# Odd layer of a two-block model: values and gates in one 512-column product, and the queries of the next pair moved

## The chip, the cores and the metric

The kernel runs on one core of one Trainium2 chip. The metric is the device time of one execution in microseconds (us); less is better. A core has TensorE (PE) for matrix products, VectorE (DVE) and ScalarE (ACT) for elementwise work, GpSimd (POOL), and SyncE (SP), which here only issues the loads of weights. PE has two rows in a trace, PE for the products and PEld for the loading of their stationary operands.

## The reference, cut to what matters

A first block (attention, feed-forward, gated embedding) is followed by two layers on 256 tokens of `x` and 256 tokens of a context. The change is in the second of these, the odd layer:

```python
zf_l, zb_l, i_l, q_l, g_l = jnp.split(h_lat @ w_in, idx, axis=-1)      # x's tokens: 5 x 2048 columns
zf_c, zb_c, i_c = jnp.split(h_ctx @ w_in[:, :idx[2]], idx[:2], axis=-1)  # context: 3 x 2048
for lb, z_l, z_c, reverse in ((lb_fwd, zf_l, zf_c, False), (lb_bwd, zb_l, zb_c, True)):
    k, logf = hgrn2_gates(z, lb)              # both token sets
    s_ctx = hgrn2_final_state(k_c, v_c, lf_c, s0)
    o_l, _ = hgrn2_chunk_scan(q_l, k_l, v_l, lf_l, s_ctx)
o = o * lax.rsqrt(jnp.mean(o * o, axis=-1, keepdims=True) + EPS)
return (o.reshape(b, n, HG_V) * onorm_g * jax.nn.silu(g)) @ w_out
```

There are 16 heads of 128 columns. Queries `q` and gates `g` are needed for the tokens of `x` alone, values `v` and the two forget projections `zf` and `zb` for both sets.

## The kernel before, in words

Everything is float32. A weight is split into a rounded part `whi` and a rest `wlo`, an activation into `h` and `l`, and a product is the sum of three (high by high, low by high, high by low), each a PE instruction with a 128x128 stationary operand.

**Chunks.** `Plan` lays the whole program out as a list of chunks of 1024 weight columns per partition (512 KB). SyncE loads a chunk into one of 5 `raw` buffers. ACT makes `whi` from it (L1152), DVE makes `wlo` (L1746), PE multiplies. There are 4 buffers of each, and the loops of ACT and DVE run with PE's: in their iteration for chunk c (`Engine.chunks`) they first split chunk c+3, and ACT's part of that waits until PE has finished chunk c-1. Then they call `pump()`.

**Pumps.** Small work that lies beside the products is written as generators that advance by one step at each `pump()`. PE calls `pump()` before each chunk, and in groups whose products cover 512 tokens also before each further 128 rows of the weight (L706 ff.). ACT and DVE call it once for each chunk, and a second time in such groups. In the odd layer `serial` is set, so that only the first generator of the list advances. A generator's waits on semaphores stand in the engine's own queue: what is behind them waits too.

**The odd layer** goes through 8 pairs of heads, j = 0 to 7. A group is one projection of a pair:

- `q` and `g`: 256 weight columns, x's 256 tokens moving: 96 products of 256 columns, 4 chunks
- `v` (token-major, activations stationary, weights moving): 4 blocks of 128 tokens, 192 products of 256 columns, 4 chunks
- `zf`, `zb`: 512 tokens moving, 96 products of 512 columns each, 4 chunks

The order is q0 g0 v0 zf0 zb0, then q, v, zf, g, zb for j = 1 to 7, then `w_out` in groups o0 to o3. Sums stand in PSUM banks 0 to 3, in two alternating sets. Bank 4 takes transposes and scores, 5 and 6 the states of the two heads (`ds`), 7 the outputs.

**Beside the products** runs `direction(j, d)`. It starts when `zf` (d = 0) or `zb` (d = 1) of the pair is complete. ACT takes sigmoids (L1688, L1689), then in its pumps logarithms (pump 1, L1321), exponentials (pump 3, L1329 to L1332), copies of the transposes (pumps 7 and 9, L1342). DVE scans in pump 2 (L2058 to L2071), makes the decayed keys in pump 4 (L2076, L2078, semaphore `kd`), and masks scores and combines states in pumps 8 and 10 (L2096 to L2104, semaphores `scm`, `ss`). PE's part has the steps `(9 if n else 10, 2 if d else 3, 2, 2, 3)` with n = 2j + d:

```python
        def turn(h):
            e.wait_ge(S("kd"), n + 1)
            if h:
                e.wait_ge(S("scm"), 2 * n + 1)
```

so for d = 1 `turn(0)` (L918) comes in PE's pump 10, `states(0)` (L933) in 12, `turn(1)` in 14, `outputs(0)` (L948) with `states(1)` in 16, `outputs(1)` in 19. For d = 0 they come in 10, 13, 15, 17, 20. Direction (7, 1) has steps of its own and runs in o0 and o1.

`readout(j)` follows in the next pair's `zf`: ACT squares (L1359) and takes a root (L1363), DVE a reciprocal (L2119), ACT scales the outputs into `OT` (L1368, its pump 3), PE transposes them (L977, seventh pump), DVE multiplies by norm and gate (L2127), ACT and DVE make the high and low part (L1372, L2131).

Of the kernel before, what the change touches and what calls it, by code (L numbers as in the profile page):

```python
# [13 lines left out]
D = 2048  # L14
T = 256
# [43 lines left out]


class Group:
    pass


class Plan:
# [55 lines left out]
    def modulate(self, W):

# [43 lines left out]
def schedule(A):  # L166
# [54 lines left out]
    p.rate = 0.0  # L221
    W = A["od_w_in"]
    for j in range(8):
        p.group(f"q{j}", W, 6144 + 256 * j, 256, NT, T)
        if j == 0:
            p.group(f"g{j}", W, 8192 + 256 * j, 256, NT, T)
        p.group(f"v{j}", W, 4096 + 256 * j, 256, NT, 2 * T, tm=True)
        p.group(f"zf{j}", W, 256 * j, 256, NT, 2 * T)
        if j > 0:
            p.group(f"g{j}", W, 8192 + 256 * j, 256, NT, T)  # L230
        p.group(f"zb{j}", W, 2048 + 256 * j, 256, NT, 2 * T)
    W = A["od_w_out"]
    for g in range(2):
# [71 lines left out]
class Memory:  # L305


    def __init__(self, nc, A):
# [132 lines left out]
        self.X1 = Turned(self, "half", cut(self.HCh, 0, T), cut(self.HCl, 0, T), True, hn, t)  # L441
        self.X1c = Turned(self, "half", cut(self.HCh, T, N), cut(self.HCl, T, N), True, hn, t)
        self.hV = self.sb("hV", [128, 4, 256], F32, F)
        self.hQ = self.sb("hQ", [128, 2, T], F32, F + 28)
        self.hG = self.sb("hG", [128, 2, T], F32, F + 30)
        self.hA = self.sb("hA", [128, 2, N], F32, F + 4)
        self.hB = self.sb("hB", [128, 2, N], F32, F + 8)
        self.hC = self.sb("hC", [128, 2, N], F32, F + 12)
# [50 lines left out]
        return self.LB[:, 32 + 16 * d + k:33 + 16 * d + k]  # L499

    def ds(self, h, n):
        return self.PS[5 + h][:, 128 * n:128 * n + 128]


class Engine:
# [18 lines left out]
    def chunks(self, name, prep=None, ahead=0, upto=None):  # L524

        G = self.plan.by[name]
        for j, ch in enumerate(G.chunks[:upto]):
            if prep is not None:
                prep.upto(min((G.j0 + j + 1) * G.kt - 1 + ahead, G.K - 1))
            self.upto(ch.c)  # L530
            self.pump()
            if self.serial and G.N == 512:
                self.pump()
            self.modulate(ch)
        return G
# [144 lines left out]
class Tensor(Engine):  # L680
# [80 lines left out]
    def modulate(self, ch):  # L761
# [12 lines left out]
        for l in ch.turns:  # L774
            self.ada_turn(l)

    def ada_turn(self, b):
        m, S, e = self.m, self.S, self.e
        e.wait_ge(S("ada_R"), b + 1)
        for i in range(4):  # L780
            t = e.transpose(m.PS[6 + b][:, 128 * i:128 * i + 128], m.R[b][:, 128 * i:128 * i + 128], m.ident)
        t.then_inc(S("ada_tr"), 1)
# [115 lines left out]
    def direction(self, j, d):  # L898
# [14 lines left out]
            elif d:  # L913
                e.wait_ge(S("scm"), 2 * n)
            elif j:
                e.wait_ge(S("og"), j)
# [65 lines left out]
def tensor(m, e):  # L982
# [93 lines left out]
    XQ = P.turned(m.X1)  # L1076
    works, reads = [], []
    for j in range(8):
        P.group(f"q{j}", XQ)
        if j == 0:  # L1080
            first = []
# [19 lines left out]
        P.group(f"v{j}", X)  # L1101
# [6 lines left out]
        if j:  # L1108
            P.group(f"g{j}", XQ)
# [29 lines left out]
class Scalar(Engine):  # L1139
# [211 lines left out]
    def readout(self, j):  # L1351
# [11 lines left out]
        e.activation(m.SM[:, 4:8], m.SM[:, 4:8], ACT.Sqrt).then_inc(S("rr"), 1)  # L1363
        yield
        yield
        e.wait_ge(S("ri"), j + 1)
        for i in range(4):
            a = e.activation(m.OT[:, i, :], m.PS[7][:, 128 * i:128 * i + 128], ACT.Copy, scale=m.SM[:, 4 + i:5 + i])  # L1368
        a.then_inc(S("ot"), 1)
        yield  # L1370
        e.wait_ge(S("og"), j + 1)
        e.activation(m.OH[:, 2 * j:2 * j + 2, :], m.hG[:, :, :], ACT.Copy).then_inc(S("oh"), 1)  # L1372
        yield


def scalar(m, e):
# [285 lines left out]
    def queries(j):  # L1662
        G = P.chunks(f"q{j}", X1, 2)
        e.wait_ge(S("mm"), G.done)
        if j:
            e.wait_ge(S("qd"), 2 * j)
        e.activation(m.hQ[:, :, :], PS[G.base][:, :], ACT.Copy).then_inc(S(f"set{G.s}"), 1)

    def gates(j):
        G = P.chunks(f"g{j}", X1, 2)  # L1670
        if j == 0:
            P.finish()
            X1c.upto(2)
        e.wait_ge(S("mm"), G.done)
        if j:
            e.wait_ge(S("ol"), j)
        e.activation(m.hG[:, :, :], PS[G.base][:, :], ACT.Sigmoid).then_inc(S("gs"), 1)

    def forget(j, d):
        n = 2 * j + d  # L1680
# [10 lines left out]

    works, reads = [], []
    for j in range(8):
        queries(j)
        if j == 0:
            P.beside = [rest()]
            gates(0)
# [39 lines left out]
class Vector(Engine):  # L1737
# [307 lines left out]
    def direction(self, j, d):  # L2045
# [68 lines left out]
    def readout(self, j):  # L2114
# [2 lines left out]
        e.tensor_scalar(m.SM[:, 4:8], m.SM[:, 0:4], 1.0 / 128, EPS, ALU.mult, ALU.add).then_inc(S("rm"), 1)  # L2117
        e.wait_ge(S("rr"), j + 1)
        e.reciprocal(m.SM[:, 4:8], m.SM[:, 4:8]).then_inc(S("ri"), 1)  # L2119
        yield  # L2120
        yield
        yield
        e.wait_ge(S("otr"), j + 1)
        G = self.plan.by[f"g{j}"]
        e.wait_ge(S(f"set{G.s}"), G.freed)
        for h in range(2):
            t = e.scalar_tensor_tensor(m.hG[:, h, :], m.PS[4][:, 256 * h:256 * h + 256], m.v("onorm", 2 * j + h),  # L2127
                                       m.hG[:, h, :], ALU.mult, ALU.mult)
        t.then_inc(S("og"), 1)
        e.wait_ge(S("oh"), j + 1)  # L2130
        e.tensor_tensor(m.OL[:, 2 * j:2 * j + 2, :], m.hG[:, :, :], m.OH[:, 2 * j:2 * j + 2, :].bitcast(F32),  # L2131
                        ALU.subtract).then_inc(S("ol"), 1)
        yield


def vector(m, e):
# [366 lines left out]
    def gates(j):
        G = P.chunks(f"g{j}")
        if j == 0:
            P.finish()
            X1c.upto(2)
        e.wait_ge(S("gs"), j + 1)
        e.tensor_tensor(m.hG[:, :, :], PS[G.base][:, :], m.hG[:, :, :], ALU.mult).then_inc(S(f"set{G.s}"), 1)

    works, reads = [], []
    for j in range(8):
        P.chunks(f"q{j}", X1, 2)
        if j == 0:
            e.wait_ge(S("ld_cx"), 32)
# [17 lines left out]
        works, reads = [P.direction(j, 1)], [P.readout(j)]
# [110 lines left out]
```

## Time and profile before

| | |
|---|---|
| median of 3 runs | 3124.61 us (3124.38 to 3124.99) |
| the profiled execution | 3124.67 us, its span 3122.9 us |
| PE busy | 3083.2 us, 99% of the span, 16978 products |
| DVE, ACT busy | 64%, 46% |
| mean share of the DMA engines, last third | 0.3 to 0.4 |
| odd layer, pair j = 3 (q3's start at 2521.57 to zb3's end) | 99.6 us |

The span is the stretch between the first and last record. PE's busy time includes modelled ends of products, so PE's pace is read from distances between starts. A row on a stretch has its bounds and length in us, the busy time and number of instructions of PE, PEld, DVE, ACT and POOL, TensorE's granted clock as a share of full speed, the DMA share and GB/s. A timeline row has start (us), duration (us), engine, line, operation, output<-inputs, shapes, and in brackets the engine's idle time before it and what ended that. An "xN" at the end of a timeline row stands for N instructions merged into it, each of which starts before the next row does. Weights of the odd layer arrive in 3.5 us a chunk.

### The profile page before, as it was taken

The numbers are of one execution on the slowest core, as the hardware profiler recorded it, in microseconds if no ns is written. First come the engines' busy times: TensorE is split into PE (matmuls) and PEld (weight loads), VectorE is DVE, ScalarE is ACT, GpSimd is POOL, SyncE is SP. The second block draws the span as 40 slices with busy tenths as digits, with TensorE's granted clock in tenths as the row PEclk, the third lists the DMA queues.
The fourth block names the chain that finished last, engine by engine and source line by source line (L and its number), as shares of the span: only waits on it lengthen the run. The fifth ranks groups of instructions, "written<-read, shape, count | busy, mean of one in ns | idle before, by whom it ended". The sixth has DMA issues, their size and how long they took to land.

```text
span 3122.9 us, 41500 instructions
## 1 busy us (share of the span) xinstructions
PE 3083.2 (99%) x16978; PEld 2666.3 (85%) x16978; DVE 1998.3 (64%) x2502; ACT 1422.3 (46%) x2029; POOL 97.3 (3%) x74
## 2 busy tenths in 40 slices
PE   8999999999999999999999999999999999999998
PEld 8989888888888888878888888888889999899987
DVE  6767777789888887857877755442743444443455
ACT  5344555465555554436422222232644544444454
POOL 0000003001111100000000000000000000000000
PEclk9999999999999999999999999999999999999999
DMA  8776666757667677775556555342333333333334
GB/s 302 231 248 216 208 212 216 250 179 230 213 221 225 216 251 266 254 240 197 161 170 191 178 193 179 127 150 95 103 96 104 100 108 114 102 110 97 112 131 146
DMA packets 369982, 557.59 MB, mean 179 GB/s; under 512 B 17088, under 2 KB 239296, under 8 KB 368512
## 3 DMA queue, kind: packets, MB, share of 16 engines
q1 hardware_dynamic: 366784, 540.08, 53.6%
q0 software_dynamic: 2000, 12.06, 1.0%
q8 instruction: 134, 2.20, 0.3%
q10 hardware_dynamic: 1008, 2.80, 0.2%
q14 instruction: 56, 0.46, 0.0%
HBM read 552.64 MB, written 2.23 MB: 178 GB/s over the span
## 4 chain that ended last, share of the span: by engine, by line
PE 95%; DVE 2%; ACT 1%; issue 1%; DMA 1%; ACTq 0%; DVEq 0%
PE ps L736 91%; DVE wlo L1746 1%; PE ps L933 0%; PE ps L948 0%; PE ps L938 0%; PE ps L950 0%; ACT whi L1152 0%; PE ps L807 0%; DMA CX<-in_ctx 0%; PE ps L771 0%; DVE HCl L1900 0%; PE ps L861 0%; PE ps L845 0%; PE ps L918 0%; PE ps L935 0%
## 5 line engine op out<-in xcount | busy, mean ns | idle before, releaser
L1746 DVE TENSOR_TENSOR wlo<-raw,whi 128x1024 fp32r<-128x1024 f32 (+1 forms) x823 | 1013.4, 1235 | 822.5 <-ACT whi L1152 820.6
L1152 ACT ACTIVATE whi<-raw 128x1024 fp32r<-128x1024 f32 x828 | 869.9, 1057 | 1166.5 <-PE ps L736 1150.3
L736 PE MATMUL ps<-HCh,whi 128*128 128x512 f32 (+1 forms) x1816 | 508.2, 361 | 0.0
L736 PE MATMUL ps<-HCh,wlo 128*128 128x512 f32 (+1 forms) x1816 | 500.8, 357 | 0.0
L736 PE MATMUL ps<-HCl,whi 128*128 128x512 f32 (+1 forms) x1816 | 500.3, 357 | 0.0
L736 PE MATMUL ps<-V,whi 128*128 128x512 f32 x1408 | 445.2, 398 | 0.8 <-DVE V L1902 0.8
L1763 DVE SCALAR_TENSOR_TENSOR acc<-raw_ada,S,acc 128x1024 f32<-128x1024 f32 x330 | 436.4, 1334 | 5.0 <-DMA raw_ada<-in_ada_w 4.2
L736 PEld LDWEIGHTS ps<-HCh,wlo 128*128 128x128 f32 x1816 | 323.6, 189 | 49.8
L736 PEld LDWEIGHTS ps<-HCl,whi 128*128 128x128 f32 x1816 | 323.5, 189 | 49.8
L736 PEld LDWEIGHTS ps<-HCh,whi 128*128 128x128 f32 x1816 | 319.7, 190 | 49.7 <-issue 4.2
L736 PEld LDWEIGHTS ps<-V,wlo 128*128 128x128 f32 x1408 | 265.4, 188 | 62.8
L736 PE MATMUL ps<-V,wlo 128*128 128x256 f32 x1408 | 277.4, 278 | 0.0
L736 PEld LDWEIGHTS ps<-V,whi 128*128 128x128 f32 x1408 | 215.2, 189 | 2.7 <-issue 1.7
L736 PE MATMUL ps<-whi,HCh 128*128 128x256 f32 (+1 forms) x896 | 197.7, 336 | 1.5 <-DVE HCl L1939 1.5
L736 PE MATMUL ps<-wlo,HCh 128*128 128x256 f32 (+1 forms) x896 | 191.5, 329 | 0.0
L736 PE MATMUL ps<-whi,HCl 128*128 128x256 f32 (+1 forms) x896 | 191.3, 329 | 0.0
L736 PEld LDWEIGHTS ps<-wlo,HCh 128*128 128x128 f32 x896 | 142.7, 190 | 15.3
L736 PEld LDWEIGHTS ps<-whi,HCl 128*128 128x128 f32 x896 | 142.4, 190 | 15.2
L736 PEld LDWEIGHTS ps<-whi,HCh 128*128 128x128 f32 x896 | 139.9, 190 | 14.7 <-issue 1.9
L736 PE MATMUL ps<-whi,Uh 128*128 128x512 f32 x384 | 121.3, 397 | 0.0
L736 PE MATMUL ps<-whi,Ul 128*128 128x512 f32 x384 | 118.6, 390 | 0.0
L736 PE MATMUL ps<-wlo,Uh 128*128 128x512 f32 x384 | 118.4, 390 | 0.0
(345 smaller groups left out, 3484.5 us busy)
## 6 DMA issues: line engine op xcount, KB each, us to landing
raw_ada<-in_ada_w SPq DMA_DIRECT2D x192, 512.0 KB, 4.8
raw<-in_w_up SPq DMA_DIRECT2D x176, 512.0 KB, 4.3
raw<-in_w_in SPq DMA_DIRECT2D x160, 512.0 KB, 4.0
raw<-in_od_w_in SPq DMA_DIRECT2D x160, 512.0 KB, 3.5
raw<-in_ev_w_in SPq DMA_DIRECT2D x96, 512.0 KB, 3.8
raw<-in_w_down SPq DMA_DIRECT2D x88, 512.0 KB, 5.1
raw<-in_w_out SPq DMA_DIRECT2D x32, 512.0 KB, 4.8
raw<-in_w_ple_gate SPq DMA_DIRECT2D x32, 512.0 KB, 4.6
```

What stands on the lines that cost most here:

```text
L736: mm = e.matmul(o, a, b, start=first and t == 0, stop=last, skip_group_check=True)
L1152: e.activation(m.whi[ch.i % SPLIT][:, 0:n], m.raw[ch.slot][:, 0:n], ACT.Copy).then_inc(S("hi"), 1)
L1746: e.tensor_tensor(m.wlo[ch.i % SPLIT][:, 0:n], m.raw[ch.slot][:, 0:n], m.whi[ch.i % SPLIT][:, 0:n].bitcast(F32), ALU.subtract).then_inc(S( ...
L1763: t = e.scalar_tensor_tensor(m.acc[v][:, :], w, c, m.acc[v][:, :], ALU.mult, ALU.add)
```

## The change

- For j = 1 to 7 `g` and `v` become one group (`Plan.pair`, PE's `values`) of 8 chunks of 256 weight rows by 512 columns, from an input `od_w_vg` in which the host has put the values' and the gates' columns of a pair side by side. For each 128 rows PE makes 6 products of 512 columns for x's tokens (values and gates) and 6 of 256 for the context's (values). The context's sums stand in bank 6, and both heads' states in bank 5.
- The gates are now token-major, so DVE multiplies the outputs by reciprocal and gate as it fills `OT`, before the transposes. ACT and DVE then apply the norm as they read the transposes.
- Group `q` of pair j + 1 stands where `g` of pair j stood; the order is q0 g0 v0 zf0 q1 zb0, then v, zf, q of the next pair, zb. After zf7 there is no such group.
- `hQ` and `hG` have two buffers each.
- `direction`'s steps are as before.

```diff
+            p.pair(f"v{j}", A["od_w_vg"], j)
         p.group(f"zf{j}", W, 256 * j, 256, NT, 2 * T)
-        if j > 0:
-            p.group(f"g{j}", W, 8192 + 256 * j, 256, NT, T)
+        if j < 7:
+            p.group(f"q{j + 1}", W, 4096 + 256 * (j + 1), 256, NT, T)
         p.group(f"zb{j}", W, 2048 + 256 * j, 256, NT, 2 * T)
...
-            if self.serial and G.N == 512:
+            if self.serial and G.N == 512 and (j % 2 or not G.pair):
                 self.pump()
...
+    def values(self, j, X):
...
+        for i, ch in enumerate(G.chunks):
+            self.pump()
+            e.wait_ge(S("lo_dve"), ch.n_lo)
...
+            for k in range(2):
+                kk = 2 * i + k
+                if k:
+                    self.pump()
+                for t in range(3):
+                    for b in range(2):
+                        e.matmul(m.PS[G.base + b][:, :], (X.lo if t == 1 else X.hi)(kk)[:, 128 * b:128 * b + 128],
+                                 ws[t == 2][:, k, :], start=kk == t == 0, stop=kk == NT - 1 and t == 2,
+                                 skip_group_check=True)
+                if i % 2 and not k:
+                    self.pump()
+                for t in range(3):
+                    for b in range(2):
+                        mm = e.matmul(m.PS[6][:, 256 * b:256 * b + 256],
```

ACT behind group `v`, and DVE's part that waits for it:

```diff
+            for b in range(2):
+                e.activation(m.hV[:, b, :], PS[G.base + b][:, 0:256], ACT.Copy)
+            e.activation(m.hV[:, 2:4, :], PS[6][:, :], ACT.Copy)
+            if j > 1:
+                e.wait_ge(S("ol"), j - 1)
+            for b in range(2):
+                a = e.activation(m.hG[j % 2][:, b, :], PS[G.base + b][:, 256:512], ACT.Sigmoid)
+            a.then_inc(S("gs"), 1)
...
+            e.wait_ge(S("gs"), j + 1)
+            for b in range(2):
+                t = e.tensor_tensor(m.hG[j % 2][:, b, :], PS[G.base + b][:, 256:512], m.hG[j % 2][:, b, :], ALU.mult)
+            t.then_inc(S(f"set{G.s}"), 1)
```

The readout, ACT's part and then DVE's:

```diff
-        e.wait_ge(S("ri"), j + 1)
-        for i in range(4):
-            a = e.activation(m.OT[:, i, :], m.PS[7][:, 128 * i:128 * i + 128], ACT.Copy, scale=m.SM[:, 4 + i:5 + i])
-        a.then_inc(S("ot"), 1)
...
+        e.wait_ge(S("otr"), j + 1)
+        for h in range(2):
+            a = e.activation(m.OH[:, 2 * j + h, :], m.PS[4][:, 256 * h:256 * h + 256], ACT.Copy,
+                             scale=m.v("onorm", 2 * j + h))
...
+        for i in range(4):
+            h, p = divmod(i, 2)
+            t = e.scalar_tensor_tensor(m.OT[:, i, :], m.PS[7][:, 128 * i:128 * i + 128], m.SM[:, 4 + i:5 + i],
+                                       m.hG[j % 2][:, p, 128 * h:128 * h + 128], ALU.mult, ALU.mult)
+        t.then_inc(S("ot"), 1)
...
+        e.wait_ge(S("oh"), j + 1)
         for h in range(2):
+            t = e.scalar_tensor_tensor(m.OL[:, 2 * j + h, :], m.PS[4][:, 256 * h:256 * h + 256],
+                                       m.v("onorm", 2 * j + h), m.OH[:, 2 * j + h, :].bitcast(F32), ALU.mult,
+                                       ALU.subtract)
```

## Rows read from the trace of the kernel before

**Rows 1.** Stretches, busy time by engine: one pair, then two behind or around waits.

```profile
2521.57:2621.20 99.63, 99.63 (x665) 91.75 (x664) 42.66 (x72) 46.46 (x69) 0.00 (x0) 1.00 0.34 106
...
632.10:638.70 6.60, 5.87 (x23) 5.05 (x22) 6.22 (x10) 4.17 (x8) 0.00 (x0) 0.50 0.24 69
...
3061.40:3068.20 6.80, 5.27 (x25) 4.11 (x24) 3.93 (x5) 2.63 (x3) 0.00 (x0) 1.00 0.49 164
```

**Rows 2.** Timeline of PE, end of g2 and first half of zb2.

```profile
2487.73 0.40 PE L736 MATMUL ps<-HCh,whi 128*128 128x256 f32 x2
...
2494.69 0.40 PE L736 MATMUL ps<-HCl,whi 128*128 128x256 f32 x2
2494.93 0.63 PE L736 MATMUL ps<-HCh,whi 128*128 128x512 f32 x2
...
2501.30 0.62 PE L736 MATMUL ps<-HCl,whi 128*128 128x512 f32 x2
```

**Rows 3.** Timeline of ACT from the end of zb2.

```profile
2521.77 0.60 ACT L1688 ACTIVATE hC<-ps 128x512 f32<-128x512 f32 x1 [7.29 <-PE ps L736]
...
2533.55 0.63 ACT L1329 ACTIVATE hKI<-hB 128x512 f32<-128x512 f32 x1 [2.73 <-DVE TS L2071]
...
2535.22 1.04 ACT L1152 ACTIVATE whi<-raw 128x1024 fp32r<-128x1024 f32 x1
```

**Rows 4.** Timeline of DVE in the same stretch.

```profile
2536.30 1.23 DVE L1746 TENSOR_TENSOR wlo<-raw,whi 128x1024 fp32r<-128x1024 f32 x1 [1.65 <-ACT whi L1152]
...
2538.63 0.48 DVE L2078 SCALAR_TENSOR_TENSOR hA<-hC,LB,hA 128x256 f32<-128x256 f32 x1
...
2544.81 0.35 DVE L2096 TENSOR_SCALAR hST<-ps,DEC 128x128 f32<-128x128 f32 x1 [1.07 <-PE ps L938]
2545.08 0.41 DVE L2097 TENSOR_TENSOR hSC<-ps,hgm 128x256 int32<-128x256 int32 x1
```

**Rows 5.** Timeline of PE: turn(0) of direction (2, 1), and states(0).

```profile
2540.29 0.38 PE L918 MATMUL ps<-cst,hA 128*128 128x128 f32 x2
...
2543.49 0.61 PE L933 MATMUL ps<-hV,hB 128*128 128x128 f32 x4
```

**Rows 6.** Timelines, direction (0, 0) inside zb0 (ACT, DVE, PE).

```profile
2293.86 0.60 ACT L1688 ACTIVATE hC<-ps 128x512 f32<-128x512 f32 x1 [4.32 <-PE ps L736]
...
2305.92 0.48 DVE L2078 SCALAR_TENSOR_TENSOR hA<-hC,LB,hA 128x256 f32<-128x256 f32 x1
...
2312.09 0.71 PE L933 MATMUL ps<-hV,hB 128*128 128x128 f32 x4 [0.23 <-ACT hB L1342]
...
2321.27 0.49 PE L948 MATMUL ps<-hST,hQD 128*128 128x128 f32 x2 [1.30 <-DVE hST L2104]
```

**Rows 7.** Timelines of ACT, DVE, PE, readout in zf3 (zf3's first product at 2560.78).

```profile
2560.98 1.09 ACT L1704 ACTIVATE hV<-ps 128x512 f32<-128x512 f32 x2 [5.53 <-PE ps L736]
...
2564.06 1.28 ACT L1363 ACT_TABLE_LOAD   x1
2565.36 0.21 ACT L1363 ACTIVATE SM<-SM 128x4 f32<-128x4 f32 x1
...
2565.60 0.18 DVE L2119 RECIPROCAL SM<-SM 128x4 f32<-128x4 f32 x1 [1.24 <-ACT SM L1363]
...
2568.97 0.60 PE L977 MATMUL ps<-cst,hOT 128*128 128x128 f32 x4
```

**Rows 8.** Timeline of PE, its waits in o0 to o1b.

```profile
3037.42 0.44 PE L918 MATMUL ps<-cst,hA 128*128 128x128 f32 x2 [1.11 <-DVE hA L2078]
...
3066.30 0.70 PE L736 MATMUL ps<-whi,Oh 128*128 128x512 f32 x2 [1.53 <-DVE Ol L2131]
```

**Rows 9.** Timeline of PE, waits before clock drops.

```profile
631.38 0.99 PE L807 MATMUL ps<-cst,H 128*128 128x128 f32 x6 [2.85 <-DVE H L2259]
...
2212.08 1.30 PE L807 MATMUL ps<-cst,hnf 128*128 128x128 f32 x6 [1.94 <-DVE hnf L1888]
2214.67 0.66 PE L807 MATMUL ps<-cst,hnf 128*128 128x128 f32 x2 [1.29 <-DVE HCl L1900]
```

More of the change, by code:

```diff
@@ L61 @@
 class Group:
-    pass
+    pair = False
 class Plan:
@@ L119, in group, with pair @@
         return G
+    def pair(self, name, W, j):
+        G = Group()
+        G.cols, G.K, G.kt, G.N, G.tm, G.raw, G.wide, G.first = 512, NT, 2, 2 * T, True, False, False, True
+        G.j0, G.j1, G.pair = 0, 8, True
+        G.s = self.sets % 2
+        self.sets += 1
+        G.use = self.uses[G.s]
+        self.uses[G.s] += 1
+        G.freed, G.base = G.use + 1, 2 * G.s
+        G.chunks = []
+        for i in range(8):
+            rows = W[i * 256:(i + 1) * 256, 512 * j:512 * j + 512]
+            G.chunks.append(self.stream(rows.rearrange("(k p) c -> p k c", p=128), 2, 512, True, True))
+        G.done = G.chunks[-1].n
+        self.by[name] = G
     def modulate(self, W):
@@ L223, in schedule @@
     for j in range(8):
-        p.group(f"q{j}", W, 6144 + 256 * j, 256, NT, T)
         if j == 0:
-            p.group(f"g{j}", W, 8192 + 256 * j, 256, NT, T)
-        p.group(f"v{j}", W, 4096 + 256 * j, 256, NT, 2 * T, tm=True)
+            p.group("q0", W, 4096, 256, NT, T)
+            p.group("g0", A["od_w_vg"], 256, 256, NT, T, tm=True)
+            p.group("v0", A["od_w_vg"], 0, 256, NT, 2 * T, tm=True)
+        else:
+            p.pair(f"v{j}", A["od_w_vg"], j)
         p.group(f"zf{j}", W, 256 * j, 256, NT, 2 * T)
-        if j > 0:
-            p.group(f"g{j}", W, 8192 + 256 * j, 256, NT, T)
+        if j < 7:
+            p.group(f"q{j + 1}", W, 4096 + 256 * (j + 1), 256, NT, T)
         p.group(f"zb{j}", W, 2048 + 256 * j, 256, NT, 2 * T)
@@ L346, in __init__ @@
         at += 4 * ADA_SLOTS
+        self.acc_at = at
         self.acc = [self.sb(f"acc{v}", [128, 1024], F32, at + 4 * v) for v in range(2)]
@@ L443, in __init__ @@
         self.hV = self.sb("hV", [128, 4, 256], F32, F)
-        self.hQ = self.sb("hQ", [128, 2, T], F32, F + 28)
-        self.hG = self.sb("hG", [128, 2, T], F32, F + 30)
+        self.hQ = [self.sb(f"hQ{i}", [128, 2, T], F32, (F + 28, self.acc_at)[i]) for i in range(2)]
+        self.hG = [self.sb(f"hG{i}", [128, 2, T], F32, (F + 30, self.acc_at + 2)[i]) for i in range(2)]
         self.hA = self.sb("hA", [128, 2, N], F32, F + 4)
@@ L501, in ds @@
     def ds(self, h, n):
-        return self.PS[5 + h][:, 128 * n:128 * n + 128]
+        return self.PS[5][:, 256 * h + 128 * n:256 * h + 128 * n + 128]
 class Engine:
@@ L775, in modulate @@
             self.ada_turn(l)
+    def values(self, j, X):
+        m, S, e = self.m, self.S, self.e
+        G = self.plan.by[f"v{j}"]
+        e.wait_ge(S(f"set{G.s}"), G.use)
+        if j > 1:
+            old = self.plan.by[f"v{j - 1}"]
+            e.wait_ge(S(f"set{old.s}"), old.freed)
+        for i, ch in enumerate(G.chunks):
+            self.pump()
+            e.wait_ge(S("lo_dve"), ch.n_lo)
+            ws = [w[ch.i % SPLIT][:, :].rearrange("p (k c) -> p k c", k=2) for w in (m.whi, m.wlo)]
+            for k in range(2):
[12 more added lines that the diff above has]
+                        mm = e.matmul(m.PS[6][:, 256 * b:256 * b + 256],
+                                      (X.lo if t == 1 else X.hi)(kk)[:, T + 128 * b:T + 128 * b + 128],
+                                      ws[t == 2][:, k, 0:256], start=kk == t == b == 0,
+                                      stop=kk == NT - 1 and t == 2, skip_group_check=True)
+            mm.then_inc(S("mm"), 1)
     def ada_turn(self, b):
@@ L915, in turn @@
             elif j:
-                e.wait_ge(S("og"), j)
+                e.wait_ge(S("ol"), j)
             for i in range(2):
@@ L1078, in tensor @@
     for j in range(8):
-        P.group(f"q{j}", XQ)
         if j == 0:
+            P.group("q0", XQ)
             first = []
@@ L1100, in tensor @@
             X.turn = XC.turn
-        P.group(f"v{j}", X)
+            P.group("v0", X)
+        else:
+            P.values(j, X)
         P.finish(*works)
@@ L1107, in tensor @@
         P.beside += works
-        if j:
-            P.group(f"g{j}", XQ)
+        if j < 7:
+            P.group(f"q{j + 1}", XQ)
         P.group(f"zb{j}", X)
@@ L1365, in readout @@
         yield
-        e.wait_ge(S("ri"), j + 1)
-        for i in range(4):
-            a = e.activation(m.OT[:, i, :], m.PS[7][:, 128 * i:128 * i + 128], ACT.Copy, scale=m.SM[:, 4 + i:5 + i])
-        a.then_inc(S("ot"), 1)
         yield
-        e.wait_ge(S("og"), j + 1)
-        e.activation(m.OH[:, 2 * j:2 * j + 2, :], m.hG[:, :, :], ACT.Copy).then_inc(S("oh"), 1)
+        e.wait_ge(S("otr"), j + 1)
+        for h in range(2):
+            a = e.activation(m.OH[:, 2 * j + h, :], m.PS[4][:, 256 * h:256 * h + 256], ACT.Copy,
+                             scale=m.v("onorm", 2 * j + h))
+        a.then_inc(S("oh"), 1)
         yield
@@ L1664, in queries, with gates @@
         e.wait_ge(S("mm"), G.done)
[L1665 to L1673, printed above, removed]
+        if j > 1:
+            e.wait_ge(S("qd"), 2 * j - 2)
+        e.activation(m.hQ[j % 2][:, :, :], PS[G.base][:, :], ACT.Copy).then_inc(S(f"set{G.s}"), 1)
+    def gates():
+        G = P.chunks("g0", X1, 2)
+        P.finish()
+        X1c.upto(2)
         e.wait_ge(S("mm"), G.done)
-        if j:
-            e.wait_ge(S("ol"), j)
-        e.activation(m.hG[:, :, :], PS[G.base][:, :], ACT.Sigmoid).then_inc(S("gs"), 1)
+        e.activation(m.hG[0][:, :, :], PS[G.base][:, :], ACT.Sigmoid).then_inc(S("gs"), 1)
     def forget(j, d):
@@ L1693, in scalar @@
     for j in range(8):
-        queries(j)
         if j == 0:
+            queries(0)
             P.beside = [rest()]
-            gates(0)
+            gates()
         G = P.chunks(f"v{j}", X1c, 2)
@@ L1702, in scalar @@
             e.wait_ge(S("om"), 4 * j)
-        for i in range(2):
-            a = e.activation(m.hV[:, 2 * i:2 * i + 2, :], PS[G.base + i][:, :], ACT.Copy)
-        a.then_inc(S(f"set{G.s}"), 1)
+            for b in range(2):
+                e.activation(m.hV[:, b, :], PS[G.base + b][:, 0:256], ACT.Copy)
+            e.activation(m.hV[:, 2:4, :], PS[6][:, :], ACT.Copy)
+            if j > 1:
+                e.wait_ge(S("ol"), j - 1)
+            for b in range(2):
+                a = e.activation(m.hG[j % 2][:, b, :], PS[G.base + b][:, 256:512], ACT.Sigmoid)
+            a.then_inc(S("gs"), 1)
+        else:
+            for i in range(2):
+                a = e.activation(m.hV[:, 2 * i:2 * i + 2, :], PS[G.base + i][:, :], ACT.Copy)
+            a.then_inc(S(f"set{G.s}"), 1)
         forget(j, 0)
@@ L1709, in scalar @@
         P.beside += works
-        if j:
-            gates(j)
+        if j < 7:
+            queries(j + 1)
         forget(j, 1)
@@ L2082, in direction @@
         e.wait_ge(S(f"set{G.s}"), G.freed)
-        e.tensor_tensor(m.QD[:, :, :], m.hQ[:, :, :], m.QD[:, :, :], ALU.mult).then_inc(S("qd"), 1)
+        e.tensor_tensor(m.QD[:, :, :], m.hQ[j % 2][:, :, :], m.QD[:, :, :], ALU.mult).then_inc(S("qd"), 1)
         yield
@@ L2119, in readout @@
         e.reciprocal(m.SM[:, 4:8], m.SM[:, 4:8]).then_inc(S("ri"), 1)
+        e.wait_ge(S("ri"), j + 1)
+        G = self.plan.by[f"v{j}" if j else "g0"]
+        e.wait_ge(S(f"set{G.s}"), G.freed)
+        for i in range(4):
[3 more added lines that the diff above has]
+        t.then_inc(S("ot"), 1)
         yield
@@ L2122, in readout @@
         yield
-        e.wait_ge(S("otr"), j + 1)
-        G = self.plan.by[f"g{j}"]
-        e.wait_ge(S(f"set{G.s}"), G.freed)
+        e.wait_ge(S("oh"), j + 1)
         for h in range(2):
[L2127 to L2132, printed above, removed]
+            t = e.scalar_tensor_tensor(m.OL[:, 2 * j + h, :], m.PS[4][:, 256 * h:256 * h + 256],
+                                       m.v("onorm", 2 * j + h), m.OH[:, 2 * j + h, :].bitcast(F32), ALU.mult,
+                                       ALU.subtract)
+        t.then_inc(S("ol"), 1)
         yield
@@ L2501, in rest, with gates @@
         yield
[L2503 to L2509, printed above, removed]
+    def gates():
+        G = P.chunks("g0")
+        P.finish()
+        X1c.upto(2)
+        e.wait_ge(S("gs"), 1)
+        e.tensor_tensor(m.hG[0][:, :, :], PS[G.base][:, :], m.hG[0][:, :, :], ALU.mult).then_inc(S(f"set{G.s}"), 1)
     works, reads = [], []
     for j in range(8):
-        P.chunks(f"q{j}", X1, 2)
         if j == 0:
+            P.chunks("q0", X1, 2)
             e.wait_ge(S("ld_cx"), 32)
@@ L2520, in vector @@
             P.beside = [rest()]
-            gates(0)
-        P.chunks(f"v{j}", X1c, 2)
+            gates()
+        G = P.chunks(f"v{j}", X1c, 2)
         P.finish(*works)
+        if j:
+            e.wait_ge(S("gs"), j + 1)
+            for b in range(2):
+                t = e.tensor_tensor(m.hG[j % 2][:, b, :], PS[G.base + b][:, 256:512], m.hG[j % 2][:, b, :], ALU.mult)
+            t.then_inc(S(f"set{G.s}"), 1)
         P.chunks(f"zf{j}", X1c, 2)
@@ L2528, in vector @@
         P.beside += works
-        if j:
-            gates(j)
+        if j < 7:
+            P.chunks(f"q{j + 1}", X1, 2)
         P.chunks(f"zb{j}")
@@ L2631 @@
         "w_ple_gate": a["w_ple_gate"][0], "ada_w": a["ada_w_2"], "ev_w_in": a["ev_w_in_2"][0],
-        "ev_pool_w": a["ev_pool_w_2"][0], "ev_w_out": a["ev_w_out_2"][0], "od_w_in": a["od_w_in_2"][0],
+        "ev_pool_w": a["ev_pool_w_2"][0], "ev_w_out": a["ev_w_out_2"][0],
+        "od_w_in": np.concatenate([a["od_w_in_2"][0][:, 0:4096], a["od_w_in_2"][0][:, 6144:8192]], axis=1),
+        "od_w_vg": np.stack([a["od_w_in_2"][0][:, 4096:6144].reshape(D, 8, 256),
+                             a["od_w_in_2"][0][:, 8192:10240].reshape(D, 8, 256)], axis=2).reshape(D, 4096),
         "od_w_out": a["od_w_out_2"][0],
```

## The prediction

> **What bounds the kernel now.** I read the page first: PE is busy for 99% of the span, DVE for 64%, ACT for 46% (the table above has them). A busy share that includes modelled ends doesn't say that nothing can be gained, so I went to one pair of the odd layer: in 99.6 us PE is busy for all of it at full clock, with DVE and ACT below half and the DMA engines at a third [rows 1]. So here the order and pace of PE's own instructions set the time, and anything on ACT or DVE counts only where PE waits for it. Then the timelines. The reader is to see three things: how far apart products start, how late ACT and DVE hand over what `direction` needs, and at which pump PE asks for it.
>
> **Products.** In g2, 256 columns wide, 29 pairs of products lie between 2487.73 and 2494.69: 0.240 us a pair, 120.0 ns each. In zb2, 512 wide, 14 pairs lie between 2494.93 and 2501.30: 227.5 ns each [rows 2]. Two products of 256 take 240 ns and one of 512 takes 227.5. Per pair of heads g's 96 and half of v's 192 (x's tokens), 192 products of 256, become 96 of 512. That saves 96 x 12.5 ns = 1.2 us, and over the 7 pairs that change **-8.4 us**. Columns, bytes, splits (20 chunks a pair) and pumps in all (56 a pair for PE) stay as they were.
>
> The Trainium skill (TensorE: Matmul & The Clock Gate, "Back-to-back issue gap") gives a gap of N/2.4 + 2.5 ns, so a fixed 2.5 ns a product, against some 13 ns in the rows above. By that rule the saving would be an estimated 1.7 us; the rows decide.
>
> **First hand-over, d = 1.** I set t = 0 at the first product behind zb (2521.57 for j = 2). ACT's sigmoids start at 0.20, the exponentials wait for DVE's scans and start at 11.98, and ACT's next split follows at 13.65 [rows 3]. DVE's split waits for that one (14.73), and only then come the decayed keys, whose last ends at 2539.11, t = 17.54 [rows 4]. A waiting product starts 0.05 behind it: so did the one in o0, where PE came early [rows 8]. Before, PE asks in pump 10: 4 chunks of q are 96 x 0.120 = 11.5 us, and five of v's 128-row steps of 12 x 0.120 = 1.44 make 18.7; the transpose starts at 2540.29, t = 18.72 [rows 5]. So there is a cover of 1.1 us. It is all that hides the chain.
>
> After the change v stands directly behind zb. A 128-row step is 6 x 227.5 + 6 x 120 ns = 2.085 us, a chunk 4.17. Pumps come at steps 0 and 1 of an even chunk, at 0, in the middle of step 0, and at 1 of an odd one: five in two chunks. Pump 10 is step 1 of chunk 3, seven steps in: t = 14.60. The chain is no shorter. ACT and DVE have pump 1 in chunk 0, pumps 2 and 3 in chunk 1, pump 4 in chunk 2, and behind the scans there is still chunk 2's split on both before pump 4: exponentials at 12.0, splits, keys done at 17.5. PE waits 17.59 - 14.60 = **3.0 us**, and all products stand behind it. Seven times: **+21.0**.
>
> **Second hand-over, d = 1.** `turn(1)` is pump 14, the middle of step 0 of chunk 5, 1.37 us into it. It waits for the mask of the scores, which DVE makes in pump 8, in chunk 5 too, behind the split made there. From a chunk's start: ACT's split starts at about 0.20 (as the sigmoids do behind zb), DVE's 1.08 later, the work behind it 1.15 later, the mask is done 0.68 on (2544.81 to 2545.49) [rows 3, 4]. With 0.05 that is 3.16, a wait of **1.8 us**. Before, DVE's pump 8 lay in v's second chunk and PE's pump 14 in the third, and DVE waited 1.07 for PE. Seven times: **+12.6**. States(0), between the two, needs ACT's copy at about 1.7 us after chunk 4's start and comes at 2.1: no wait, by 0.4 us. `outputs` have chunks of room.
>
> **Readout.** ACT now makes hV in three copies and then loads sigmoid's table and does two sigmoids of 256 columns before the squares: 1.28 for the load, about 0.8 for the rest. The root moves from 4.38 us after hV's start to about 6.5, the reciprocal ends 0.42 later, four DVE products of about 0.3 make 8.2; PE's transposes start at 7.99 [rows 7]. I take a wait of 0.3, **+2.1** in all; with shorter DVE products it is nothing, with 0.4 each it is 0.7 (+4.9). DVE waits for the gates in front of zf's first split, which PE needs three chunks later: covered. ACT's four scalings leave a path that had no wait.
>
> After a table load the next activation starts 1.30 behind the load's start (2564.06, 2565.36) [rows 7]. The Trainium skill (ScalarE: Activation LUTs, "What ACT_TABLE_LOAD costs") puts 1.38 us of drain on top; by that the readout's wait would be 1.4 us longer, an estimated 10 us in all. The rows show none of it.
>
> **The ends of the layer.** Direction (0, 0) lay inside zb0 alone, with waits of 0.23 and 1.30 [rows 6]; q1 now lies before it: -1.5. Direction (7, 0) gets that place, since there is no q8, and asks one pump earlier. With two pumps a chunk the chain is shorter (2293.86 to 2306.40, 12.5 us; with 0.20 before it 12.8 against PE's 9 steps of 1.365 = 12.3): a wait of 0.5, then 0.23 + 1.37 = 1.6 for the copy, then the 1.3: +3.4. In readout 7, high part and low part now read the transposes, so DVE no longer makes `hG` between them: 1.53 of wait before o0b [rows 8] falls by about 1.4. Together **+0.5**. The wait of 1.11 in o0 stays.
>
> Queries: the copy's wait for `qd` goes with two buffers of `hQ`. It came when DVE had the keys done, and PE waited for none of what ACT did next: 0. d = 0 has q and zb in front of it as it had g and zb: 11.5 + 5 x 1.365 = 18.3 against 17.6, no wait. DMA: same bytes, a third busy, chunks loaded five ahead: 0.
>
> Sum of the plain terms: -8.4 + 21.0 + 12.6 + 2.1 + 0.5 = **+27.8**.
>
> **The clock.** A wait of 2.85 us was followed by a granted clock of 0.50 of full speed, the level of 1.2 GHz, for some 6.7 us, and a wait of 1.94 with one of 1.29 behind it was followed by one too; behind one of 1.53 the clock stayed at 1.00 [rows 1, 8, 9]. The trace's idle time is some 0.2 shorter than a delay, because products' ends are modelled late, so my delays of 3.0 and 1.8 would read 2.8 and 1.6. The first is in the range that brought a drop both times. At half speed a step of 2.085 takes twice the streaming time, about 3.85, so 6.7 us do the work of 3.6: 3.1 us lost each time. How many of 7 is open: none to seven (0 to +21.7), and a few of the second kind might do it too (up to +9). Two of two is thin, and one of those waits came in two parts; I take five, **+15.5**.
>
> Result: +43.3 on the profiled execution's 3124.67, which is the median of the runs within 0.1: 3168, and a little off for overlaps of a drop with the wait that starts it: **3167**.
>
> **Rivals.**
> - **Clock holds** (0 or 1 drops): 3124.6 + 27.8 + 0 to 3 = 3152 to 3156. For it: only two cases in the trace, neither in this layer.
> - **Only one of the two hand-overs waits.** Only the first, with four drops: 3124.6 + 15.2 + 12.4 = 3152. Only the second: 3124.6 + 6.8 = 3131. For it: the second rests on DVE's order split, then pump; against it: that order is in the rows.
> - **Faster.** The chain through ACT and DVE is done by t = 14.6 and the mask within 1.37 us of chunk 5. Then the products decide: -8.4 + 2.1 + 0.5 and no wait = 3119; without the readout's wait 3117. The point is 14.6 us: direction (0, 0) did the chain in 12.5, but with no split between exponentials and keys [rows 6], and here chunk 2's split is in between. Against: 17.3 us from sigmoids to keys, in all pairs alike.
> - **More drops**, behind nearly all first and some second waits: 3124.6 + 27.8 + 21.7 + 6 = 3180.
>
> **How the numbers follow.** Both waits and two to six drops, 0.60 (3158 to 3172); clock holds 0.12; one hand-over alone 0.10 (a third of it near 3131); more drops 0.10; neither wait 0.08. What a measurement of this kernel can tell from no change is 0.2%, 6 us. Faster by more 0.07, within 0.03, slower 0.90. The range, 3146 to 3181, takes in the case of a clock that holds and most of the one with more drops, and leaves out the third of the single hand-over and the case without waits, with a few per cent beyond the top.
>
> **What the profile after would show.** In v1 to v7 the chunks' 512- and 256-wide products at 227 and 120 ns. PE's transposes at L918's counterpart idle for about 2.8 us on DVE's hA, 7 times, and again for about 1.6 on DVE's hSC, 7 times; DVE's keys 17.5 us behind zb. Drops of the clock to 0.50 in v, about five. The prediction is wrong if the keys are done before seven steps, if a 512-wide product beside 256-wide ones costs more than 227 ns, or if the clock holds.

## The result, and the profile after

The changed kernel takes **3159.23 us** (median of 4 runs, 3158.38 to 3159.58) against 3124.73 for the kernel before, measured beside it: a ratio of 1.0109, 95% interval 1.0096 to 1.0122. It is 34.5 us slower, clear of noise, the way that was forecast (3167) and inside the range. The profiled execution's span is 3157.8 us, 34.9 more than before.

The page after: busy time and instructions of each engine, then what the chain that ended last is made of. The third line is that chain in the kernel before.

```profile
PE 3087.2 (98%) x16306; PEld 2635.9 (83%) x16306; DVE 2000.4 (63%) x2533; ACT 1425.7 (45%) x2026; POOL 97.2 (3%) x74
...
PE 91%; DVE 4%; ACT 3%; issue 1%; DMA 1%; ACTq 0%; DVEq 0%
...
PE 95%; DVE 2%; ACT 1%; issue 1%; DMA 1%; ACTq 0%; DVEq 0%
```

PE has 672 products fewer (7 x 96), as intended, and is busy for longer. DVE and ACT now hold 7% of the chain that sets the end, where they held 3%. The waits of PE behind 2300 us. Each line has who waited, for whom, the us in all, how often, and the longest:

```profile
PE ps L969 <- DVE hA L2136: 18.8, 8, 2.8
PE ps L969 <- DVE hSC L2155: 12.4, 7, 1.8
PE ps L984 <- ACT hB L1395: 1.6, 1, 1.6
PE ps L999 <- DVE hST L2162: 1.3, 1, 1.3
```

L969 is the transpose in `turn` (L918 before), L2136 the keys, L2155 the mask. In the kernel before, this stretch had four waits of PE of 0.2 to 1.5 us each. The first line is seven waits in v1 to v7 (1.85, then six of 2.76) and one of 0.38 in zb7; the second is one in each of v1 to v7. They are where they were expected. PE's timeline in v3 shows the pace and the first wait:

```profile
2542.72 0.63 PE L815 MATMUL ps<-whi,HCh 128*128 128x512 f32 x2
...
2553.22 0.63 PE L815 MATMUL ps<-whi,HCh 128*128 128x512 f32 x2
...
2555.08 0.40 PE L822 MATMUL ps<-wlo,HCh 128*128 128x256 f32 x2
2558.24 0.44 PE L969 MATMUL ps<-cst,hA 128*128 128x128 f32 x2 [2.76 <-DVE hA L2136]
...
2570.91 0.41 PE L969 MATMUL ps<-cst,hA 128*128 128x128 f32 x2 [1.77 <-DVE hSC L2155]
```

The reader is to see three things. Five steps of 128 rows lie between 2542.72 and 2553.22: 2.100 us each. The last products before the wait start at 2555.08 and 2555.20 and would have made way at 2555.32, and the transpose starts at 2558.24: a delay of 2.92 for an idle time of 2.76, since the trace models the products' ends some 0.16 late. And the second wait follows 12.7 us later. DVE's timeline explains the first, with ACT's split that releases it:

```profile
2554.30 1.99 ACT L1205 ACTIVATE whi<-raw 128x1024 fp32r<-128x1024 f32 x2
```

```profile
2555.38 1.23 DVE L1804 TENSOR_TENSOR wlo<-raw,whi 128x1024 fp32r<-128x1024 f32 x1 [2.78 <-ACT whi L1205]
...
2557.71 0.48 DVE L2136 SCALAR_TENSOR_TENSOR hA<-hC,LB,hA 128x256 f32<-128x256 f32 x1
...
2568.94 1.23 DVE L1804 TENSOR_TENSOR wlo<-raw,whi 128x1024 fp32r<-128x1024 f32 x1 [4.20 <-ACT whi L1205]
...
2570.35 0.41 DVE L2155 TENSOR_TENSOR hSC<-ps,hgm 128x256 int32<-128x256 int32 x1
```

v3 starts at 2540.65, and the keys end at 2558.19: 17.54 us behind, to the hundredth what [rows 3, 4] had shown before the change. DVE had stood idle for 2.78 us in front of a split that nobody needed soon; the keys stand behind it. The mask at 2570.76 ends behind chunk 5's split in the same way.

Where PE resumes, the clock is lower in five of the seven groups (from 2453.21, 2559.03, 2664.84, 2873.05 and 2978.86, in v2, v3, v4, v6 and v7). Stretches of the changed kernel: all of v3 and of v5, the 0.7 us behind v3's wait and the 3.4 behind that, and the 3.4 behind v5's wait:

```profile
2540.65:2585.37 44.72, 40.19 (x235) 35.28 (x234) 17.71 (x31) 16.82 (x22) 0.00 (x0) 0.96 0.29 91
2751.14:2794.30 43.16, 38.63 (x236) 34.02 (x234) 17.70 (x31) 16.82 (x22) 0.00 (x0) 1.00 0.31 95
...
2558.30:2559.00 0.70, 0.70 (x5) 0.66 (x6) 0.70 (x2) 0.00 (x0) 0.00 (x0) 1.00 0.94 301
2559.03:2562.43 3.40, 3.40 (x12) 2.92 (x12) 0.90 (x1) 0.01 (x1) 0.00 (x0) 0.50 0.53 167
...
2769.10:2772.50 3.40, 3.40 (x20) 2.93 (x19) 1.31 (x2) 1.03 (x2) 0.00 (x0) 1.00 0.48 152
```

v3 and v5 do the same work with the same two waits. v3 has 3.4 us at half speed (12 products where v5 has 20) and takes 1.56 us longer: the price of one drop, against the 3.1 that [rows 1] with twice the length had suggested.

The books on the spans, each from starts in the two timelines:

| | us |
|---|---|
| paired group's steps, 7 x 16 x (2.100 - 18 x 0.120) | -6.7 |
| first wait, idle 18.4, with 0.16 each for modelled ends | +19.5 |
| second wait, idle 12.4, likewise | +13.6 |
| five drops of the clock at 1.56, the difference of v3 and v5 | +7.8 |
| waits of zb0 gone, those of zb7 new (0.38, 1.59, 1.29) | +1.9 |
| waits in o0 and before o0b gone [rows 8] | -2.6 |
| start of the odd layer (2214.98 before, 2215.82 after), not touched | +0.8 |
| sum, against 34.9 measured | +34.3 |

### The profile page after: what moved, and what is told of

Its sections match the earlier page's. It is cut to its first block, busy times and chain, and to the rows that moved or that the text cites. A ratio compares the mean times of both kernels' runs of the same rounds, so it can differ in the third digit from the quotient of the medians.

```text
span 3157.8 us, 40169 instructions
## 1 busy us (share of the span) xinstructions
PE 3087.2 (98%) x16306; PEld 2635.9 (83%) x16306; DVE 2000.4 (63%) x2533; ACT 1425.7 (45%) x2026; POOL 97.2 (3%) x74
## 4 chain that ended last, share of the span: by engine, by line
PE 91%; DVE 4%; ACT 3%; issue 1%; DMA 1%; ACTq 0%; DVEq 0%
PE ps L756 82%; PE ps L815 3%; PE ps L822 2%; ACT whi L1205 1%; DVE wlo L1804 1%; PE ps L984 0%; PE ps L989 0%; PE ps L999 0%; PE ps L1001 0%; DMA CX<-in_ctx 0%; PE ps L791 0%; PE ps L858 0%; ACT hA L1374 0%; PE ps L969 0%; DVE hB L2116 0%
## 5 line engine op out<-in xcount | busy, mean ns | idle before, releaser
L756 PE MATMUL ps<-HCh,whi 128*128 128x512 f32 (+1 forms) x1560 | 456.4, 374 | 0.0
L756 PE MATMUL ps<-HCh,wlo 128*128 128x512 f32 (+1 forms) x1560 | 449.3, 369 | 0.0
L756 PE MATMUL ps<-HCl,whi 128*128 128x512 f32 (+1 forms) x1560 | 448.9, 369 | 0.0
L756 PEld LDWEIGHTS ps<-HCh,whi 128*128 128x128 f32 x1560 | 279.6, 189 | 49.3 <-issue 4.2
L756 PE MATMUL ps<-whi,HCh 128*128 128x512 f32 (+1 forms) x480 | 129.5, 376 | 1.5 <-DVE HCl L1997 1.5
L756 PE MATMUL ps<-wlo,HCh 128*128 128x512 f32 (+1 forms) x480 | 125.8, 368 | 0.0
L756 PE MATMUL ps<-whi,HCl 128*128 128x512 f32 (+1 forms) x480 | 125.8, 368 | 0.0
L756 PE MATMUL ps<-whi,ACh 128*128 128x512 f32 x352 | 108.7, 390 | 0.0
L756 PE MATMUL ps<-wlo,ACh 128*128 128x512 f32 x352 | 108.4, 389 | 0.0
L756 PE MATMUL ps<-whi,ACl 128*128 128x512 f32 x352 | 108.4, 389 | 0.0
```

The source lines that it names most:

```text
L756: mm = e.matmul(o, a, b, start=first and t == 0, stop=last, skip_group_check=True)
```

## The experiments

The theory: PE asks for what `direction` gives before ACT and DVE can have it, because their pumps stand behind splits, and the pause then costs clock. The rival: the new group itself, its wider products or its shared banks, costs the time.

**Ask later.** Only PE's steps for d = 1, on the changed kernel:

```diff
-            steps = (9 if n else 10, 2 if d else 3, 2, 2, 3)
+            steps = (11, 1, 2, 2, 3) if d else (9 if n else 10, 3, 2, 2, 3)
```

> The changed kernel with PE's steps for d = 1 at (11, 1, 2, 2, 3): turn(0) in pump 12, nine steps of 2.10 us in (18.9 us against keys at 17.5), turn(1) in pump 15, 3.3 us into its chunk against a mask at 3.2. Late hand-overs theory: both waits go (33 us) and with them the clock drops (5 x 1.56 us), 3159.2 - 33.1 - 7.8 = 3118, some 6 us below the kernel before. Rival, the new products or the shared banks cost the time: above 3140. Rival, the waits only move on to states or outputs: between 3125 and 3150, with a new row of PE waiting for hB or hST.

Measured: **3118.71 us**, ratio to the kernel before 0.9981 (0.9971 to 0.9990). No wait is left in v1 to v7, and the clock stays up in v3, which takes 38.41 us instead of 44.72:

```profile
2529.81:2568.22 38.41, 38.41 (x235) 34.17 (x234) 17.71 (x31) 16.93 (x22) 0.00 (x0) 1.00 0.35 106
```

The schedule alone gives back 40.5 us, more than the change had lost. The group, its products and its banks are as in the change, so the rival falls. The cover that is left is thin: in v3 the second `turn` starts at 2554.43, 0.15 behind the end of the mask (2553.87 + 0.41), as it does where PE waits.

**The second wait alone.** `(9, 2, 3, 2, 3)` for d = 1.

> The changed kernel with d = 1 at (9, 2, 3, 2, 3): turn(0) as in the change, turn(1) and what follows one pump later. Late hand-overs theory: the 7 waits for hSC (1.94 us each as delays) go, those for hA stay at 2.8, clock drops stay (five, give or take two at 1.56 us): 3159.2 - 13.6 = 3146 (3142 to 3149). Rival, the second wait is only a consequence of the first: it would have gone together with the first alone, and here stays or moves on: 3155 or more.

Measured: **3151.24 us** (ratio 1.0086, 1.0071 to 1.0101), outside both. The row in v3:

```profile
2570.13 0.41 PE L969 MATMUL ps<-cst,hA 128*128 128x128 f32 x2 [1.07 <-DVE hSC L2155]
```

The wait shrank from 1.78 to 1.07 and didn't go. The error was mine: I had counted `states(0)`, 1.1 us, between chunk 5's start and pump 15, but it lies in chunk 4. Pump 15 comes one step, 2.10 us, into the chunk, where pump 14 comes 1.39 into it, and the mask is done at 3.16 or 3.17 in both: 0.71 less. Seven times 0.71 make -5.0. The clock dropped three times in the profiled execution and not five, -3.1, so that 3159.6 - 8.1 = 3151.5 against its 3152.0. So the second wait has its own cause, the split in chunk 5, and doesn't hang on the first. In *ask later* it had gone because there `states(0)` itself lies in pump 13, at chunk 5's start, so that its 1.0 us and a step of 2.18 stand in front of `turn(1)`: 3.2.

**The other side of the hand-over.** PE's steps stay, ACT and DVE take their second pump in even chunks:

```diff
-            if self.serial and G.N == 512 and (j % 2 or not G.pair):
+            if self.serial and G.N == 512 and (j % 2 == 0 or not G.pair):
```

> The changed kernel, PE's steps untouched; ACT and DVE take their two pumps of the paired group in the even chunks, not the odd ones. Then the scans come before chunk 1's split, pump 8 in chunk 4 and not 5. Late hand-overs theory: keys at about 15.1 us instead of 17.5, PE's first wait falls from 2.9 to about 0.5, the second goes, no drops: 3159.2 - 17 - 13.6 - 7.8 = 3121. Rival, the chain is as long as its own instructions whatever the pumps: the first wait stays at 2.8: about 3140 or more.

Measured: **3119.42 us** (0.9983, 0.9973 to 0.9992). DVE's timeline in v3, which starts at 2529.74:

```profile
2535.18 0.69 DVE L2116 TENSOR_TENSOR_SCAN hB<-cst,hA 128x256 f32<-128x256 f32 x1 [0.98 <-ACT hA L1374]
...
2538.88 1.22 DVE L1804 TENSOR_TENSOR wlo<-raw,whi 128x1024 fp32r<-128x1024 f32 x1
...
2544.08 0.47 DVE L2136 SCALAR_TENSOR_TENSOR hA<-hC,LB,hA 128x256 f32<-128x256 f32 x1
```

The scans start as soon as the logarithms are there, one split earlier than in the change, and the keys are done at 14.8 us, not 17.5. PE's transpose starts at 2544.61, with no idle time in the trace, though some 0.2 behind the end of its step (0.5 was expected). The 2.7 us came from one pump's place in front of a split; the instructions of the chain are the same. A late consumer and an early producer cure the same two waits.

**The old kernel, made to ask early.** `(6, 5, 2, 2, 3)` for d = 1 in the kernel before.

> The kernel before, d = 1 at (6, 5, 2, 2, 3): turn(0) in pump 7 instead of 10, 14.4 us behind zb, all else in place. Late hand-overs theory: the wait of the change appears in the old kernel, 3.2 us seven times (+22), with clock drops behind some (about five, +8 if they are 3.4 us long each): 3155 (3147 to 3162). Rival, the new group causes the loss: 3125.

Measured: **3154.18 us** (1.0092, 1.0077 to 1.0107). PE's row in v3 of the old kernel:

```profile
2544.42 0.44 PE L918 MATMUL ps<-cst,hA 128*128 128x128 f32 x2 [3.04 <-DVE hA L2078]
```

```profile
2545.90:2549.10 3.20, 3.20 (x17) 3.20 (x16) 1.22 (x1) 0.70 (x1) 0.00 (x0) 0.50 0.06 11
2856.50:2863.10 6.60, 5.81 (x27) 5.81 (x28) 2.57 (x4) 1.54 (x2) 0.00 (x0) 0.50 0.41 133
```

Six waits of 3.0 (the one in v1 is 0.24) are 18.4 us of idle time, with 0.16 each for modelled ends 19.5, and there are drops behind or around five, four of 3.4 us and one twice as long: 19.5 + 4 x 1.56 + 3.1 = 28.8 on 3124.95 is 3153.8. The loss of the change can be had without the change.

**Width of the products.** On the *ask later* kernel, each product of 512 columns as two of 256:

```diff
-                    for b in range(2):
-                        e.matmul(m.PS[G.base + b][:, :], (X.lo if t == 1 else X.hi)(kk)[:, 128 * b:128 * b + 128],
-                                 ws[t == 2][:, k, :], start=kk == t == 0, stop=kk == NT - 1 and t == 2,
+                    for b in range(4):
+                        b, c = b // 2, slice(256 * (b % 2), 256 * (b % 2) + 256)
+                        e.matmul(m.PS[G.base + b][:, c], (X.lo if t == 1 else X.hi)(kk)[:, 128 * b:128 * b + 128],
+                                 ws[t == 2][:, k, c], start=kk == t == c.start == 0, stop=kk == NT - 1 and t == 2,
```

Beside it, *ask later* once more as the base:

> The retimed kernel of the run ask_later once more, beside the next ones, as their base: 3118.7, no waits in v1 to v7, no clock drop in the layer.

> As ask_later, but each product of 512 columns in the paired group is made as two of 256 (values, then gates). Every other thing is as there. By the pace in the trace of the change, a step of 2.100 us (512 beside 256) against 18 x 0.120 = 2.160: 7 x 16 x 0.060 = +6.7, 3125.4. Rival, the wider product gives the 8.4 of the forecast: 3127. Rival, width doesn't matter, the gain over the kernel before came from elsewhere: 3119.

Measured, on one chip: base **3119.00 us** (0.9980, 0.9971 to 0.9989), narrow **3125.17** (1.0000, 0.9991 to 1.0008): +6.2. The narrow steps:

```profile
2540.35 0.64 PE L816 MATMUL ps<-whi,HCh 128*128 128x256 f32 x4
...
2542.51 0.64 PE L816 MATMUL ps<-whi,HCh 128*128 128x256 f32 x4
...
2544.67 0.64 PE L816 MATMUL ps<-whi,HCh 128*128 128x256 f32 x4
```

2.160 us a step. So the wider product is all that the change is seen to give, and all else in it (order of groups, token-major gates, two buffers), with the later asking, is worth nothing that this measurement can tell (3 us either way).

**The clock alone.** The changed kernel with products in front of `turn(0)`'s wait, for d = 1 and n < 15; their sums are never read:

```diff
+            if d and h == 0 and n < 15:
+                e.wait_ge(S("scm"), 2 * n)
+                for i in range(FILL):
+                    e.matmul(PS[4][:, :], m.HCh[:, 0, 0:128], m.HCh[:, 0, :], start=True, stop=True,
+                             skip_group_check=True)
```

> The changed kernel with its early asking, and 12 products of 512 columns that nobody reads, into bank 4, in front of turn(0)'s wait for d = 1 in v1 to v7. They take 2.73 of the 2.92 us for which PE would stand still, and end before the keys are done. Clock theory: the wait stays as lost time but PE isn't idle, so no drop: 3159.2 - 7.8 = 3151.4. Rival, the drops cost nothing beyond the waits: 3159. Rival, the fill makes the keys late: above 3160.

Measured: **3152.24 us** (1.0086, 1.0072 to 1.0100), 7.0 below the change. PE is as late as before but busy:

```profile
2554.08 2.91 PE L965 MATMUL ps<-HCh 128*128 128x512 f32 x12
2556.99 0.44 PE L975 MATMUL ps<-cst,hA 128*128 128x128 f32 x2
```

From the start of v2 to that of v3 in this kernel, then the same in the changed kernel, and there from v5 to v6:

```profile
2435.67:2539.40 103.73, 101.95 (x581) 88.61 (x580) 43.06 (x76) 47.16 (x69) 0.00 (x0) 1.00 0.33 102
...
2435.39:2540.65 105.26, 100.72 (x569) 87.74 (x568) 43.05 (x76) 47.14 (x69) 0.00 (x0) 0.98 0.32 101
...
2751.14:2854.82 103.68, 99.15 (x569) 86.48 (x568) 43.04 (x76) 47.14 (x69) 0.00 (x0) 1.00 0.33 102
```

In *filled* all seven stretches from one v to the next read 1.00. The filled pair takes as long as a pair of the changed kernel in which the clock held, and 1.5 us less than one with a drop. Only in v1 do the products cost time themselves: PE would have waited there for 2.0 us, and the fill takes 2.75. The drops' 7.8 less that 0.7 is 7.1, against the 7.0 measured. The seven waits of 1.78 for the mask are still in it, and no drop follows any of them.

**Both ends.** *Ask later*, and `9 if n % 14 else 10` for d = 0, so that direction (7, 0) asks one pump later.

> As ask_later, and direction (7, 0) asks one pump later (10 steps, as direction (0, 0)). The wait of 0.38 for hA goes, that for hB falls from 1.59 to about 0.2, that of 1.29 for hST stays: -1.9, 3116.8. Rival, the wait moves to the end of zb7, since its 16 pumps don't hold the 21 steps: 3118.7.

Measured: **3116.63 us** (0.9973, 0.9962 to 0.9983), the fastest kernel here, 0.27% below the kernel before. PE's waits behind 2230 us:

```profile
PE ps L999 <- DVE hST L2162: 1.3, 1, 1.3
PE ps L858 <- DVE hnf L1946: 0.5, 1, 0.5
PE ps L858 <- DVE HCl L1958: 0.3, 1, 0.3
PE ps L984 <- ACT hB L1395: 0.2, 1, 0.2
```

2.4 us below its base, where 1.9 were expected; the runs of each kernel spread by some 1.5.

## Why the prediction was right, and where its terms were off

**Both hand-overs** were right in place, cause and, but for small parts, size. The first was +21.0 and is +19.5: in v1 PE waits 1.85, since `direction(0, 0)` ends in a burst between zb0 and v1, during which ACT's sigmoids already run; the other six are 2.92 each as delays, where 2.99 were said. The second was +12.6 and is +13.6: in v3 the mask is done 3.17 us into the chunk, where 3.11 were said, and the transpose starts 0.15 behind it and not 0.05.

**Products** were -8.4 and are -6.7. The 227.5 ns of [rows 2] hold between products of one width; six of 512 and six of 256 in turn take 15 ns a step more. That is one of the signs that the prediction had named for being wrong; it came, at 1.7 us in all. The *narrow* run gives nearly the same size by itself, 6.2.

**Clock.** The mechanism was right and its size was not. Five drops were taken, and five came. The number is luck in part: it was a guess between none and seven, and *second later*, with the same seven first waits, had three. The term priced each drop at 6.7 us of half speed, from the two drops in the trace before, and here each lasted 3.4: 1.56 us lost and not 3.1, so +7.8 and not +15.5. This is the largest error, and nearly all of the 8 us between 3167 and 3159. *Filled* shows the term by itself: 7.1 of its size were to come back and 7.0 did. One of the two cases in the trace before was also misread: the clock was at 0.50 from 2212.4 on, behind the wait of 1.94 and before the one of 1.29 [rows 9], which so had no part in the drop:

```profile
2212.40:2214.67 2.27, 0.98 (x7) 0.61 (x4) 2.27 (x7) 2.05 (x5) 0.00 (x0) 0.50 0.00 0
```

The Trainium skill (TensorE: Matmul & The Clock Gate, "HAM oscillation") has a kernel whose clock falls again in the gap of each iteration, a wait of about 3 to 5 us. The traces here agree in kind, with pauses of 2.76 us, but the clock fell behind five of seven and not behind each. What a drop costs had to come from a row.

**Readout** was +2.1 and is nothing: the reciprocals' and gates' four products take 1.13 us, `OT` is full 8.0 us behind hV's start, just as PE comes for it, and PE's transposes start without idle time. **The ends** were +0.5 and are -0.7: zb7's waits came as said (0.38, 1.59, 1.29), and the burst that they force between zb7 and o0 gives ACT 4.2 us of start instead of 0.2, so that the wait of 1.11 in o0, said to stay, went too. Two figures of the Trainium skill that were weighed in the prediction were not seen. By the 2.5 ns of a product's gap (TensorE: Matmul & The Clock Gate, "Back-to-back issue gap") the saving was an estimated 1.7 us, and it was 6.7. By the drain behind a table load (ScalarE: Activation LUTs, "What ACT_TABLE_LOAD costs") the readout was to lose an estimated 10 us, and its wait was nothing: in zf3 the load starts at 2586.73 and the sigmoid behind it at 2588.02, 1.29 later.

**Rivals.** "Clock holds" is *filled*; it didn't come by itself. "Faster" needed the keys by 14.6 us: *pumps even* did it with 14.8, by one swapped pump, and its 3119.4 is where that rival had put the time (3117 to 3119). It needed another order of pumps, not less work.

## What to carry to other kernels

In a kernel whose stages are tied by counts of steps and not by time, a change of step length moves the consumer against the producer. Work out, for each wait, when the consumer asks and when the producer can have it, in microseconds from a common start; here a cover of 1.1 us stood against a shift of 4.1. The producer's time is set by what stands in front of it in its queue: one pump moved in front of a split that was not urgent brought the keys 2.7 us earlier. And judge the change only when this is mended: the same group is 1.1% slower with old step counts and 0.2% to 0.3% faster with new ones.

## What the runs showed of the hardware

- A pause of 2.76 us in PE was followed by half clock in 5 of 6 cases in the changed kernel and in 2 of 6 in *second later*, one of 3.03 in 5 of 6, one of 1.85 in one of two. None of the fourteen of 1.78 in the change and in *filled* was. The same pause in the same code has it in one pair and not in the next (v3 and v5 above), and a shorter one can have it where a longer one has not:

```profile
2350.30:2353.60 3.30, 3.30 (x11) 2.73 (x10) 1.29 (x2) 0.00 (x0) 0.00 (x0) 0.50 0.50 155
2455.00:2458.40 3.40, 3.40 (x20) 2.89 (x19) 1.25 (x3) 1.17 (x2) 0.00 (x0) 1.00 0.52 166
```

These are *second later*, behind a wait of 1.85 and behind one of 2.76.
- Drops come in two lengths, 3.4 and 6.8 us, and the length doesn't go by the code: behind the wait of 2.85 at 631 us (2.86 in the changed kernel), in code that the change doesn't touch, the kernel before was at half clock for 6.6 us and more [rows 1], the changed one for 3.4. What decides between them was not tried.

```profile
633.95:637.30 3.35, 3.35 (x12) 2.96 (x13) 3.26 (x7) 1.49 (x3) 0.00 (x0) 0.50 0.00 0
637.40:640.70 3.30, 2.87 (x19) 2.40 (x17) 3.30 (x5) 2.45 (x5) 0.00 (x0) 1.00 0.63 178
```

- Products of 512 columns next to products of 256 cost 15 ns in a step of twelve: 2.100 us, against 6 x 227.5 + 6 x 120 ns = 2.085. It isn't that here the weights move and the activations stand still: so they do in `w_out`, where products of 512 columns alone start 226.8 ns apart, 14 pairs between these rows of the changed kernel:

```profile
3109.78 0.62 PE L756 MATMUL ps<-whi,Oh 128*128 128x512 f32 x2
...
3116.13 0.62 PE L756 MATMUL ps<-wlo,Oh 128*128 128x512 f32 x2
```
